# Two triangular products of a recurrent pair, cut from whole squares into an upper and a lower part

## What is computed

```python
def _rwkv7_step(S, inp):
    r, w, k, v, a, b = inp
    sa = jnp.einsum('bhvk,bhk->bhv', S, a)
    S = S * w[:, :, None, :] + sa[..., None] * b[:, :, None, :] + v[..., None] * k[:, :, None, :]
    y = jnp.einsum('bhvk,bhk->bhv', S, r)
    return S, y
...
    xs = tuple(jnp.moveaxis(u, 1, 0) for u in (r_h, w_h, k_h, v_h, -kk, kk * i_h))
    s_new, y = lax.scan(_rwkv7_step, s0.astype(jnp.float32), xs)
```

## Time and profile before

| | |
|---|---|
| median of 3 runs | 4158.36 us (4155.36 to 4164.71) |
| the profiled execution | 4158.62 us |
| its span, first to last instruction | 4156.8 us |
| mean granted TensorE clock | 0.983 of full speed |
| PE busy | 3955.0 us, 95% of the span |
| PEld busy | 3499.0 us, 84% |
| DVE busy / ACT busy / POOL busy | 2014.5 / 1420.0 / 289.3 us |

### The profile page before, as it was taken

How to read it: one execution, slowest core, us unless ns; L and a number is a source line. 1 busy time by engine, 2 the same in 40 slices (tenths; PEclk the granted TensorE clock), 3 DMA queues, 4 the chain that set the end, 5 groups by cost and what they waited for, 6 DMA issues and landing times.

```text
span 4156.8 us, 84432 instructions
## 1 busy us (share of the span) xinstructions
PE 3955.0 (95%) x36004; PEld 3499.0 (84%) x36004; DVE 2014.5 (48%) x3239; ACT 1420.0 (34%) x2345; POOL 289.3 (7%) x463
## 2 busy tenths in 40 slices
PE   7999999999999998999989999999998999989998
PEld 6888888888876687999978888888888766979997
DVE  4544554554345545333355455555443455554344
ACT  4333344343322323222243333444333223232222
POOL 1000000000111021000000000000001110100000
PEclk9999999999999999999999999999999999999998
DMA  6222221222466473443332222222224665412222
GB/s 206 66 60 70 71 74 61 68 66 78 134 204 214 157 243 112 122 134 107 117 109 68 61 71 69 72 63 69 68 76 134 204 208 162 156 46 76 70 73 71
DMA packets 476464, 446.09 MB, mean 107 GB/s; under 512 B 18766, under 2 KB 408968, under 8 KB 475216
## 3 DMA queue, kind: packets, MB, share of 16 engines
q1 hardware_dynamic: 417136, 251.74, 20.0%
q0 software_dynamic: 41568, 155.70, 11.6%
q10 hardware_dynamic: 17408, 33.56, 2.2%
HBM read 344.48 MB, written 96.45 MB: 106 GB/s over the span
## 4 chain that ended last, share of the span: by engine, by line
PE 85%; DVE 8%; ACT 3%; issue 2%; DMA 2%; DVEq 0%; ACTq 0%; POOL 0%; SPq 0%
PE ps L803 82%; DVE scr L2062 4%; PE ps L807 3%; ACT scr L1496 2%; DVE h_lo L2062 1%; DVE w_lo L2075 1%; DMA scr<-in_ada_w_dram 1%; ACT w_hi L1509 1%; DVE lw L2062 1%; DVE scr L2064 0%; ACT L1496 0%; ACT scr L1649 0%; DMA scr<-in_x_sample_dram 0%; DVE acc L2062 0%; DMA w_raw<-in_w_ffn_down_dram 0%
## 5 line engine op out<-in xcount | busy, mean ns | idle before, releaser
L803 PE MATMUL ps<-h_hi,w_hi 128*128 128x320 f32 x4544 | 1105.0, 325 | 75.1 <-DVEq L2070 23.8
L803 PE MATMUL ps<-h_lo,w_hi 128*128 128x320 f32 x4544 | 1041.9, 311 | 0.0
L803 PE MATMUL ps<-h_hi,w_lo 128*128 128x320 f32 x4544 | 1041.4, 311 | 0.0
L803 PEld LDWEIGHTS ps<-h_hi,w_hi 128*128 128x128 f32 x4544 | 748.6, 190 | 163.4 <-issue 133.7
L803 PEld LDWEIGHTS ps<-h_lo,w_hi 128*128 128x128 f32 x4544 | 767.0, 190 | 0.0
L803 PEld LDWEIGHTS ps<-h_hi,w_lo 128*128 128x128 f32 x4544 | 766.1, 189 | 0.0
L803 PE MATMUL ps<-scr 64*64 64x64 f32 (+10 forms) x13248 | 679.3, 250 | 22.0 <-DVEq L2226 11.7
L803 PEld LDWEIGHTS ps<-scr 64*64 64x64 f32 (+4 forms) x13248 | 464.3, 141 | 218.1 <-issue 163.3
L1509 ACT ACTIVATE w_hi<-w_raw 128x1024 fp32r<-128x1024 f32 (+1 forms) x468 | 411.0, 878 | 685.0 <-PE ps L803 667.3
L2075 DVE TENSOR_TENSOR w_lo<-w_raw,w_hi 128x1024 fp32r<-128x1024 f32 (+1 forms) x468 | 469.5, 1003 | 252.5 <-ACT w_hi L1509 232.0
L1496 ACT ACTIVATE scr<-ps 128x256 f32<-128x256 f32 (+7 forms) x899 | 377.4, 420 | 573.1 <-PE ps L803 380.6
(11 more groups left out here) (155 smaller groups left out, 3010.8 us busy)
## 6 DMA issues: line engine op xcount, KB each, us to landing
w_raw<-in_w_in_dram SPq DMA_DIRECT2D x180, 512.0 KB, 3.8
scr<-in_ada_w_dram POOLq DMA_DIRECT2D x40, 1024.0 KB, 6.2
scratch_z<-scr SPq DMA_DIRECT2D x124, 320.0 KB, 2.2
scr<-in_state_ret_dram POOLq DMA_DIRECT2D x64, 512.0 KB, 4.9
out_dram<-scr ACTq DMA_DIRECT2D x64, 512.0 KB, 3.1
w_raw<-in_w_ffn_up_dram SPq DMA_DIRECT2D x64, 512.0 KB, 4.0
w_raw<-in_w_ffn_down_dram SPq DMA_DIRECT2D x128, 256.0 KB, 2.7
scr<-scratch_z POOLq DMA_DIRECT2D x24, 1280.0 KB, 9.0
```

The costliest lines, as they stand in the source:

```text
L803: return pe.matmul(out, lhsT, rhs, start=start, stop=stop, skip_group_check=True)
```

## The change

Each of the two sets of ten products becomes twenty, without the zero quarter. A product with `r == 0` takes the upper 64 rows of the stationary matrix and all its 128 columns; one with `r == 1` takes the lower 64 rows and columns 64 to 127 only, and writes to PSUM partitions 64 to 127 alone, onto what the first wrote. Head `q` = 0 goes to the first bank and head `q` = 1 to the second. The order is: the five upper ones of head 0; then, block by block, an upper one of head 1 and a lower one of head 0; then the five lower ones of head 1. With z now in banks 5 and 6 by heads, ScalarE's copy reads 320 columns of each.

```diff
-            def flat(bank, c, n):
-                return ps[:, bank + c // 512, c % 512:c % 512 + n]
+            def lower_products(bank, mats, moving, first):
+
+                def rows(r, b, q):
+                    out = ps[64 * r:128, bank + q, 64 * b:64 * b + 64]
+                    return mm(out, mats[half(r), 2 * b + q, 64 * r:128], moving(b, q)[half(r)], first and r == 0 and b == 0, r == 1)
+                for b in range(NBLK):
+                    rows(0, b, 0)
+                for b in range(NBLK):
+                    rows(0, b, 1)
+                    rows(1, b, 0)
+                for b in range(NBLK):
+                    last = rows(1, b, 1)
+                return last
...
-                for m in range(2 * NBLK):
-                    last = mm(flat(5, 64 * m, 64), AKT[:, m], TOKB[:, 4 * (m // 2) + 3, half(m % 2)])
+                last = lower_products(5, AKT, lambda b, q: TOKB[:, 4 * b + 3, half(q)], True)
                 M(last, "pe_in", "z")
...
-                for m in range(2 * NBLK):
-                    b, q = m // 2, m % 2
-                    mm(ps[:, 2 + q, 64 * b:64 * b + 64], XTF[:, m], Z_[:, m], b == 0, True)
+                lower_products(2, XTF, lambda b, q: Z_[:, 2 * b + q], True)
...
-                do(Z_.rearrange("p m n -> p (m n)"), five_blocks(5))
+                do(Z_.rearrange("p (b q) n -> p q b n", q=2), ps[:, 5:7, 0:64 * NBLK].rearrange("p q (b n) -> p q b n", n=64))
```

## The result

The changed kernel takes 4309.84 us in the median of four runs (4305.47 to 4321.39), the kernel before 4160.55 in four (4155.36 to 4164.71). The ratio is 1.036, with a 95% interval of 1.0344 to 1.0376: 149 us more, outside the forecast range. The forecast was 4244, and slower.

What follows compares the result with a forecast made beforehand. TensorE's instruction stream was taken as the bound. z costing 2.75 us more and the second set 2.66 made 5.41 a pair, 86.6 for 16; added to 4158.6, 4245, stated as 4244; range 4180 to 4265.

Steps and rivals of the forecast that it cites:

- The bound: Whole kernel: time is what TensorE's instruction stream takes, TensorE being busy for 95% of the span.
- the unit price: Passes of both sets: time goes with columns loaded, 0.112 us for 128 and 0.058 for 64, whatever the rows.
- One side remark: Weight loads: the skill's estimate, 107 ns for 128 columns, would alter no term of the sum by over 5%.
- The changes of shape: Nine inside each set, between 64 by 128 and 64 by 64: array runs empty at each, 0.15 to 0.21 us.
- The set inside: Twenty products of a set, without entry and exit: 4.70 us, against 2.07 in the second set before.
- entry to third filling product: Around z, from last filling product ahead to third behind: 5.49 us against 2.74, so 2.75 more.
- Rival 1: Inside both sets: no emptying between the two shapes, so 24.5 us more in all, 4183; chance 0.14.
- rivals 3 and 4: Both sets: lone half-height loads cheaper, 8 us shorter, 4151, chance 0.03; or nothing visible, weaker saving, 4158, chance 0.03.
- rival 2: In the sets: clock falls to 0.50 as well, 1.7 us per set, 54 us more, 4298; chance 0.08.
- as empty as 304 us was: Around 304 us PE was empty for most of two microseconds, then the clock was 0.50 for some three and a half.
- The copies: ScalarE's copy of z: reading 320 columns from each of two banks costs nothing more, 0.70 us against 0.71.
- the waits: PE's waits in the pairs, 1.4 us each: no new wait, and none of the possible 22 us taken back.

Runs made afterwards that it cites:

- z_one_shape: Kernel before with the change at z only, lower products as wide as upper ones, on PSUM banks of their own, their sums left out: 4187.42 us.
- two_runs: Changed kernel with all ten upper products first, then all ten lower ones, one change of shape inside a set for nine: 4241.15 us.
- more_columns: Changed kernel with each upper product streaming its 64 moving columns twice, the extra into PSUM columns nothing reads: 4316.28 us.
- two_runs_more: two_runs with each upper product streaming its 64 columns twice, the second time into PSUM columns nothing reads: 4208.58 us.
- quarter_alone: Kernel before with 30 idle products ahead of z, all on the array's first 64 by 64 tile: 4214.55 us.

## Why the prediction was wrong, step by step

**The bound and the unit price held.** A pass costs its load's columns and not its rows: twelve upper passes start within 1.28 us, 0.112 apart after the first, and the whole set fits with 0.058 for the lower ones. No gain from the zero quarter was to be had, since twenty passes still load 128 columns. One side remark was off: with the load time that the prediction quotes, the 0.58 us of the lower five would be 8% less, not under 5%; no term of the sum goes by it.

**The changes of shape held, in place and size.** The set inside was forecast at 4.70 us and is 4.63; entry to third filling product 5.49 and 5.43. The second set is 4.63 inside for 2.07 before, 2.56 more, with 0.03 at its ends by the forecast. In place of the forecast's 86.6 us for all pairs that is (2.69 + 2.59) x 16 = 84; the sets that ran wholly at 1.00 give 85. z_one_shape and two_runs show by removal that it is these changes. Rival 1 (no emptying) is out, and rivals 3 and 4 with it.

**The step that failed is rival 2, the clock,** given a chance of 0.08 and told as "a few falls (up to eight, 14 us) I count within my own range". Not a few sets but 28 of 32 had lower clock in them or right behind, and it stayed down into what follows; the sign that the prediction gave for this rival, 0.50 inside pairs that read 1.00, is there. By the medians 149 - 84 = 65 us are over; in the profiled pair of executions the lower clock costs 78 us, less 8 that come back in waits. With 319 - 141 = 178 us more at the lower clock, that is some 0.4 us lost for each microsecond at it. The argument that the reader was given against rival 2 was that "the sets of today, half streaming, keep 1.00". That row was of sets of 2.1 us over the full array. Nothing in the trace of before showed what a stretch of twice that length, half streaming through half of the rows, would do, and I had worked out for the middle 4 x 0.055 of 0.63 us, little more than a third, and still did not put it in the sum. The size of rival 2 (54 us over the sum, 4298) was near, 12 us short as a term of the likeliest case. Its condition was only part of the story: it asked for a middle as empty as 304 us was, and two_runs lost the clock in most sets with no such middle.

**What remains open.** That the lower clock took the 65 us is counted in the traces; what lets the clock fall is shown by an experiment for two_runs alone. For the changed kernel's own order no variant kept that order and held the clock (more_columns was meant to and did not), so that its gaps and half-empty passes are the reason is argued from z_one_shape and two_runs_more. Why some sets keep 1.00 and most do not, in one and the same order, is not settled either.

**The copies held, and the waits nearly.** ScalarE's copy of z takes 0.70 us from two banks, and in the pair shown PE's waits are the same to a tenth. Over the whole kernel 8 us of waiting came back, where the forecast took none.

## What to carry to other kernels

For short float32 products count the passes by the columns that each loads, and look for tiles that load side by side; leaving out a zero block that does not shorten the load saves nothing, and two column halves of the full matrix took 34 us off. Mixed tile widths in one run cost 1.1 us for eight changes here, 0.14 each, so keep one shape, or sort by shape. When an edit stretches a sparse part of TensorE's stream, put the clock into the sum and not only into the rivals: look in the clock column at what the nearest stretch of that length and sparseness did, and at what runs behind it, since that pays too.

## What was not expected of the hardware

- Doubling the moving columns of a product made the kernel 33 us faster (two_runs_more 4208.58, two_runs 4241.15), because the clock held.
- The clock held over 3.5 us of passes on one 64 by 64 tile in all 16 places (quarter_alone), and fell over or behind 20 of the 32 sets of two_runs, 3.5 us of passes of which some three fifths of the time are 64 by 128 ones that stream half of the time.
- Four times as many passes on four tiles cost 41 us more than on one, with waits of up to 3.0 us that the profile puts down to issue alone.
